# Six early gate tiles instead of ten, none of them in the first attention, which gets a fourth score bank

## What is computed

```python
p = _split_in(x @ w_in[l])
ya = _mixer_a(p["a_q"], p["a_k"], p["a_v"], rpb_table[:, :A_HEADS])
yb = _mixer_b(...)
yc = _mixer_c(...)
yd = _mixer_d(...)
ys = jnp.stack([ya, yb, yc, yd], axis=2)
gates = jax.nn.sigmoid(p["gate"].reshape(bsz, seq, N_BRANCHES, D_MODEL))
merged = jnp.sum(gates * jnp.einsum('bsnc,ncd->bsnd', ys, w_branch[l]), axis=2)
x = _layer_norm(DN_ALPHA * x + merged @ w_out[l], ln_g[l, 0], ln_b[l, 0])
```

## Time and profile before

| what | value |
|---|---|
| median of 3 runs | 2735.7 us (2730.84 to 2739.39) |
| the profiled execution's own time | 2739.49 us |
| its span, first to last instruction | 2737.7 us |
| PE busy | 2591.2 us, 95% of the span |
| DVE busy | 1083.1 us, 40% |
| ACT busy | 793.0 us, 29% |
| POOL busy | 953.7 us, 35% |

### The profile page before, as it was taken

The page is one execution under the profiler, slowest core; times in us unless marked ns, Lnnn a source line. Parts: engine busy times, 40 slices in busy tenths (PEclk is TensorE's granted clock), DMA queues, the critical chain, the costliest instruction groups (busy, mean ns, idle before and its releaser), DMA issues. The chain is left out here.

```text
span 2737.7 us, 30875 instructions
## 1 busy us (share of the span) xinstructions
PE 2591.2 (95%) x12456; PEld 1936.9 (71%) x12456; DVE 1083.1 (40%) x1764; ACT 793.0 (29%) x1128; POOL 953.7 (35%) x313
## 2 busy tenths in 40 slices
PE   8878789999889999899999999999998999999998
PEld 6666578788433336675888888887765888888886
DVE  4765454445421113376444421122276444311111
ACT  3024321322211113426222332222327223322311
POOL 4564100244123332320444444444320444444443
PEclk9988899899989999999999999999999999999999
DMA  4421010232669995340322222222340222222223
GB/s 167 155 108 70 31 39 1 100 108 93 250 248 388 389 385 216 108 101 7 108 93 94 100 99 92 95 106 92 114 93 17 94 106 93 93 92 106 94 93 123
DMA packets 83021, 339.46 MB, mean 124 GB/s; under 512 B 34262, under 2 KB 34646, under 8 KB 47296
## 3 DMA queue, kind: packets, MB, share of 16 engines
q1 hardware_dynamic: 63640, 315.24, 31.7%
q10 hardware_dynamic: 5416, 13.82, 1.4%
q0 software_dynamic: 13824, 8.44, 1.0%
HBM read 379.99 MB, written 28.74 MB: 149 GB/s over the span
## 5 line engine op out<-in xcount | busy, mean ns | idle before, releaser
L167 POOL TENSOR_TENSOR w_lo<-w_raw,w_hi 128x2048 fp32r<-128x2048 f32 x150 | 698.8, 4658 | 1333.7 <-ACT w_hi L160 1314.8
L193 PE MATMUL bank<-xh,w_hi 128*128 128x512 f32 x1784 | 709.4, 398 | 35.3 <-DVE w_lo L399 11.1
L194 PE MATMUL bank<-xl,w_hi 128*128 128x512 f32 x1784 | 698.6, 392 | 0.0
L195 PE MATMUL bank<-xh,w_lo 128*128 128x512 f32 x1784 | 698.3, 391 | 0.0
L193 PEld LDWEIGHTS bank<-xh,w_hi 128*128 128x128 f32 x1784 | 337.7, 189 | 120.4 <-issue 31.3
L160 ACT ACTIVATE w_hi<-w_raw 128x2048 fp32r<-128x2048 f32 x152 | 290.4, 1911 | 378.3 <-PE bank L193 356.2
L194 PEld LDWEIGHTS bank<-xl,w_hi 128*128 128x128 f32 x1784 | 337.7, 189 | 74.0 <-issue 5.0
L195 PEld LDWEIGHTS bank<-xh,w_lo 128*128 128x128 f32 x1784 | 337.5, 189 | 70.8
L193 PE MATMUL bank<-ha,w_hi 128*128 128x512 f32 x480 | 186.7, 389 | 0.0
L194 PE MATMUL bank<-hb,w_hi 128*128 128x512 f32 x480 | 186.7, 389 | 0.0
L195 PE MATMUL bank<-ha,w_lo 128*128 128x512 f32 x480 | 186.7, 389 | 0.0
(11 more groups left out here) (588 smaller groups left out, 3758.3 us busy)
## 6 DMA issues: line engine op xcount, KB each, us to landing
w_raw<-weights SPq DMA_DIRECT2D x189, 1024.0 KB, 4.8
ring<-weights SPq DMA_DIRECT2D x49, 1024.0 KB, 9.9
before_halves<-weights SPq DMA_DIRECT2D x18, 1024.0 KB
res<-weights SPq DMA_DIRECT2D x16, 1024.0 KB
distance_bias<-distance_bias_once ACTq DMA_DIRECT2D x8, 512.0 KB
na_bias<-grid_bias SPq DMA_DIRECT2D x16, 240.0 KB, 6.7
strips<-distance_bias SPq DMA_DIRECT2D x8, 448.0 KB, 4.0
ring<-picked_rows SPq DMA_DIRECT2D x6, 512.0 KB, 6.4
```

The lines of the kernel that those rows point to most:

```text
L167: engine.tensor_tensor(self.lo[:, s, :], self.raw[:, s, :], self.hi[:, s, :].bitcast(F32), ALU.subtract).then_inc(self.split, 1)
L193: self.released(pe.matmul(out, hi, moving[0], start=start, stop=False))
L194: pe.matmul(out, hi, moving[1], start=False, stop=False)
L195: return pe.matmul(out, lo, moving[0], start=False, stop=stop)
```

## The change

- The list of early tiles goes from ten (0, 3, 6, 9, 12 and the same plus 16) to six (0, 5, 10 and the same plus 16). The merge so makes 26 gate tiles instead of 22, and the stream holds 3 early chunks instead of 5.
- The first attention has no gate work on any engine, and four score banks.
- `mixer_c` rounds (ACT) and splits (POOL) the first two tiles in the stage ahead of `head_norm`; `head_norm` still makes one tile on PE, and no longer rounds or splits one.
- The first stage of `mixer_d` still makes two tiles.
- The second stage of `mixer_d` (L1622) makes three tiles instead of two: 24 blocks on PE, two splits on POOL instead of one, one more rounding and one more copy on ACT, three stores on SP.
- The tiles go to banks 6 and 7 in turn.

```diff
-EARLY_GATES = (0, 3, 6, 9, 12)
+EARLY_GATES = (0, 5, 10)
...
-        n_scores = 3 if gates else 4
+        n_scores = 4
...
-                if gates and s in (5, 7):
-                    gates.move(sp, 1)
-            if gates:
-                gates.move(sp, 3)
...
-                if gates:
-                    gates.fill(pe, (3, 3, 2, 0)[s % 4])
...
-            if gates:
-                gates.prepare(act)
...
-                if gates and s % 4 == 3:
-                    gates.copy(act, 1, then_prepare=s < 19)
...
-                gates.subtract(pool, 2)
-                shift(pool, Order(pool, pool_order), lambda n: gates.subtract(pool, n))
-                gates.subtract(pool, 6)
+                shift(pool, Order(pool, pool_order))
...
-                gates.subtract(pool, 7)
+                gates.subtract(pool, 2)
...
                     act.activation(g, g, ACT.Silu).then_inc(silu_ready, 1)
+                k.gates.prepare(act)
...
+            @block.gpsimd
+            def _(pool):
+                k.gates.subtract(pool, 2)
...
-                k.gates.subtract(pool, 9)
+                k.gates.subtract(pool, 4)
...
-                k.gates.fill(pe, 16)
+                k.gates.fill(pe, 24)
...
-                k.gates.move(sp, 2)
+                k.gates.move(sp, 3)
...
-                k.gates.subtract(pool, 10)
+                k.gates.subtract(pool, 6)
...
                     k.gates.copy(act, 1, then_prepare=p == 0)
+                k.gates.copy(act, 1)
...
-                             [7 if j < 5 else 6 + j % 2 for j in range(len(EARLY))], gate_dram)
+                             [6 + j % 2 for j in range(len(EARLY))], gate_dram)
```

More of the change, by code:

```diff
@@ L861, in root_programs, with attention @@
     return names, dict(tensor=tensor, scalar=scalar, scalar_end=scalar_end, vector=vector)
-def attention(k, units, outs, probt, strip_loads=(), gates=None, kept=None, shift=None, decays=None):
+def attention(k, units, outs, probt, strip_loads=(), kept=None, shift=None, decays=None):
     steps = len(units) // 2
@@ L1397, in mixers_ab, with shift @@
     with memory(k, strips=(4, STRIP), moved=(SEQ,)) as (strips, moved):
-        def shift(pool, step, between):
+        def shift(pool, step):
             for j, t in enumerate([T1["dr"], T1["dr"] + 1, T1["dk"], T1["dk"] + 1, T1["dv"], T1["dv"] + 1, T1["low"]]):
@@ L1405, in shift @@
                 step(pool.tensor_tensor(z, sh, z, ALU.add))
-                if j == 4:
-                    between(3)
         tiles = [slice(128 * t, 128 * t + 128) for t in range(4)]
@@ L1428, in mixers_ab @@
                               select=select[:, i - 1, 0:n] if b and i else None, rows=rows, cols=tiles[i]))
-        attention(k, units, [yb[:, p, :] for p in range(4)], yb[:, 4:8, :], strip_loads=loads, gates=k.gates,
+        attention(k, units, [yb[:, p, :] for p in range(4)], yb[:, 4:8, :], strip_loads=loads,
                   shift=shift, decays=decays)
```

## The result

The changed kernel takes **2745.1 us**, the median of 5 runs (2743.04 to 2748.12), against 2735.7 before (5 runs by then, 2730.84 to 2739.39); the ratio is 1.0042 with a 95% interval of 1.0031 to 1.0054. Run again beside the experiments, it took 2743.9 (2739.45 to 2744.72), ratio 1.0037 [1.0023, 1.0051] to a kernel before at 2734.0. The forecast was 2736.3, no change that can be measured. The kernel became slower, by 0.4%: 8.8 us above the forecast and 9.4 above the kernel before.

What follows compares the result with a forecast made beforehand. PE was taken to bound the merge, and PE's late scores to delay VectorE in the attention. The terms 21.8 - 25 + 0.3 + 0.5 + 3.0 (`mixer_d`'s third tile) gave +0.6 us, 2736.3 us at the median; range 2727 to 2747.

Steps and rivals of the forecast that it cites:

- The merge, +21.8: Merge: four more gate tiles at 5.44 us each, all on the path; 21.8 us, bounds 20.5 and 24.
- The attention, -25: First attention: without five gate tiles, VectorE sets the pace and stops waiting for scores; saves 25 us, bounds 15 and 30.
- The 4 us for cold spells and lockstep: First attention: 4 us set against the saving for PE's half-clock spells and VectorE's waits on ACT's exponentials.
- the tail: End of the first attention: transposes, copies and value products behind VectorE's last instruction, taken as 4.2 us with hand-overs.
- half clock throughout: Rival, first attention: PE at half clock, saving only 15 us, total 2746.3; chance 0.17, alone or with lockstep.
- lockstep: Rival, first attention: VectorE waits for each ACT exponential, saving 22.3 us, total 2741; counted within the 0.77 for same.
- The fourth bank, nothing, between -1 and 0: First attention: a fourth score bank gains nothing, as PE's own order already holds it back.
- The small products, +0.3: Small products after the attention: clock may be low from the start behind a quieter PE; +0.3 us, between 0 and 1.
- Branch C's main stage, +0.5: Branch C: added roundings and POOL splits may hold back a VectorE state-chain instruction; +0.5 us, bounds 0 and 2.4.
- head_norm ... as before: 0: `head_norm`: loses a rounding and a split, but PE's tile and its copy still end the stage; 0.
- The profile's own time: Whole kernel: the profiled execution lay 3.8 us above the median, and this difference was carried to the forecast median.
- unchanged stages behind the merge, 0: Norm, routing, experts and second block behind the merge: no term in the sum, so 0.

Runs made afterwards that it cites:

- run 7: The kernel before, making all ten early tiles, but with the changed kernel's merge of 26 late gates: 2764.8 us, ratio 1.0105.
- run 4: The changed kernel with the merge of before (22 late gates), four gate tiles left out altogether: 2719.6 us, ratio 0.9941 to the kernel before.
- run 3: The changed kernel with three score banks instead of four in the first attention: 2739.9 us, ratio 1.002 to the kernel before.
- Run 6: The changed kernel with throwaway matmuls, 15 in branch C before the wait for the states and 4 behind the merge's last product: 2738.5 us, ratio 1.0017 to before.
- run 11: The kernel before with 12 throwaway matmuls at the start of the merge: 2737.1 us, ratio 1.0013.
- run 12: The changed kernel with 12 throwaway matmuls at the start of the merge: 2739.9 us, ratio 1.0022 to the kernel before.
- ten-tile version: Against the kernel before: three early tiles in the attention, one in branch C, third in `mixer_d`'s second stage, three score banks: 2727.2 and 2727.9 us.

## Why the prediction was wrong

**The merge, +21.8.** Right: +21.8 in the first profile, and +21.7 and +21.8 in runs 7 and 4. In the second profile of the changed kernel it was +19.4, with 2.3 us more in the stretch ahead of it. Both come from the clock: that stretch had more of the half clock (0.92 for 0.93 over 158 us), and the merge's first 15.4 us ran at 0.89 instead of 0.69. That the two cancel is luck.

**The attention, -25, bounds 15 and 30.** Right in kind, off by 1 to 2 us: -23.1 and -24.0. Following VectorE and subtracting its waits for PE gave the end within 1 us. The 4 us for cold spells and lockstep were used up and 0.9 more, and the tail took 1.9 us more than its rows at full clock had said. The two rivals, half clock throughout and lockstep, each happened in part: the clock of the stage is 0.71 (0.75 in the second profile) for 0.85, and PE waits 11.2 us for ACT's copies.

**The fourth bank, nothing, between -1 and 0.** No gain, as forecast, and perhaps a loss: run 3 is 4 us faster in the median, with intervals that overlap. The prediction followed the order of PE's work and didn't ask when PE idles with the bank and without.

**The small products, +0.3.** They came out at -1.7 and -0.4. The prediction had the clock the wrong way round: it expected a low clock from the start behind a quieter PE. The stretch ran at 1.00, and at 0.75 in the second profile, where the kernel before had 0.54.

**Branch C's main stage, +0.5, bounds 0 and 2.4.** Right: +0.3, with the held-back instruction of 1.92 us.

**The step that failed: "head_norm ... as before: 0", and the silence on the state products in front of it.** The stretches from the state products to the end of `mixer_d`'s first stage cost +4.8 us (+4.3 in the second pair). Their work is unchanged, so the sum had no term for them. The prediction priced the clock where the work was removed, as a rival for the attention, and let it end with that stage. But PE was done with its part of branch C's main stage sooner (busy for 10.42 us of it at 0.76, before for 12.11 at 0.63), and then had 4.08 us to wait instead of 2.11. Behind that wait the clock was 0.50 (270 to 275) and 32 products took 6.63 us for 3.79. Run 6 fills the wait and gets 3.6 to 4.1 us back. The length of the wait alone doesn't give the price: with 2.52 us in run 3 the three stretches still cost 3.4 us more than before. The Trainium skill ("TensorE: Matmul & The Clock Gate", section "HAM oscillation — how this bites in real kernels") describes this pattern, a PE that waits between groups of products and restarts at half clock; the prediction applied it to one stage. The trace agrees in the stages behind: a wait of 4.08 us, then the half clock.

**The profile's own time.** The prediction carried a difference of 3.8 us between profile and median to the result, rightly as arithmetic. It isn't the cause of the miss. What it hid was where the surplus stood: 5.8 us in the unchanged first stage.

**The rest: unchanged stages behind the merge, 0.** They took 1662.9 and 1659.5 us in the changed kernel, from the norm to the last part, against 1657.3 twice. Over all fourteen profiles this sum goes from 1657.3 to 1664.0, and by 0, 3.4 and 4.0 us between two profiles of one kernel. The kernel before has it at its lowest. Runs 6, 11 and 12 move parts of it by shifts alone. So about 2 to 6 us of the result stand in stages whose work nobody changed; runs 11 and 12 speak for them following from where the clock's spells happen to fall, which no step of the sum could have given; a term of 0 with bounds of 0 and 6 would have been right, and the chance of slower far above 0.17.

Together, for the first pair: the attention and small products came out at 0.1 us from their terms together (-24.8 for -24.7), the state products to `mixer_d` +4.8, behind the merge +5.6 less 0.1 in the last part; the first stage -0.7 and small differences in the other terms (-0.2 and -0.1) make up the difference between 9.8 and 0.6.

**The range and the rival.** The measured 2745.1 lies inside the stated range, 2727 to 2747, and close to the 2746.3 of the rival "half clock through the attention". That is luck: the attention saved 23 to 24 us and not 15, and the surplus stood in stages that the rival left at nothing.

What stays open: what decides where the spells fall. The idle stretch of PE before the norm is 1.92 us in both kernels, with the norm at 0.81 in one and at 1.00 in the other, so its length does not decide; what PE did before it may. Nor was it tried to vary the fourth bank with the clock held up.

## What to carry to other kernels

An engine that is relieved waits longer, and for PE the wait has a price behind it: after taking work off PE, look at every stage that follows before the next long busy stretch, and ask for each idle stretch of PE whether the products behind it ran at 1.00 before. Work that has to be done somewhere on PE belongs into just those waits: in branch C a gate tile of 5.45 us cost 3.2 and 3.5, while in the attention the two tiles removed had cost 6.5 each. And read two profiles of the same kernel before pricing a change of tens of microseconds that cancels: here the unchanged first stage differs by 5.8 us between two profiles of the kernel before, and all behind the merge by 4.0 us between two of the ten-tile version, where the result is 9.4.

## What the hardware showed that was not expected

- Throwaway matmuls needn't cost their time: with 19 of them the median is 5.4 us under the changed kernel's second one, with 12 at another place 4.0, though the intervals of the ratios overlap in both cases. What is shown beyond doubt is the local gain of the first, 3.6 to 4.1 us over three stages.
- Twelve throwaway matmuls that made the merge less than a microsecond longer went with a norm behind it of 8.8 us at 0.81 for 7.2 at 1.00 in one kernel and the reverse in the other, with the same 16 matmuls and the same 1.92 us of idle time before them.
- PE at half clock and then at full clock in one stage (0.50 in 255 to 260, 0.85 in 260 to 265) does its part sooner than VectorE does its own, and the gain comes back as a longer wait and another spell (0.50 in 270 to 275):

```profile
255.00:260.00 5.00, 5.00 (x29) 4.26 (x29) 2.92 (x6) 2.57 (x4) 3.30 (x2) 0.50 0.00 0
260.00:265.00 5.00, 3.70 (x38) 2.81 (x34) 4.75 (x8) 1.19 (x2) 1.35 (x1) 0.85 0.00 0
...
270.00:275.00 5.00, 4.41 (x21) 4.22 (x20) 1.17 (x2) 0.00 (x0) 0.00 (x0) 0.50 0.00 0
```
